# One encoder block on one core: u's low parts all by VectorE, tables loaded in pieces, v staged elsewhere, keys split 112 and 64

## What is computed

```python
hn = rms_norm(h, norm1_g[l])
q, k, v, u, g_na, g_ssm = jnp.split(hn @ w_in[l], IN_SPLITS, axis=-1)
y_na = neighbourhood_attention(q, k, v, na_rpb[l]).reshape(b, L, NA_WIDTH) @ w_proj_na[l]
y_ssm = s5_branch(u, ...) @ w_proj_ssm[l]
mixed = jax.nn.sigmoid(g_na) * y_na + jax.nn.sigmoid(g_ssm) * y_ssm
h = h + mixed @ w_out[l]
h = h + conv_gated_ffn(rms_norm(h, norm2_g[l]), w_up[l], conv_w[l], conv_b[l], w_down[l])
```

## Time and profile before

| | |
|---|---|
| median of 3 runs | 1456.84 us (1456.76 to 1457.27) |
| the profiled execution, its own time | 1456.88 us |
| its span, first to last instruction | 1455.0 us |
| busy: PE, DVE, ACT, POOL | 1432.3, 600.5, 663.3, 1014.2 us |
| mean granted TensorE clock | 0.997 |
| DMA | 271.48 MB, mean 187 GB/s |

### The profile page before, as it was taken

One profiled execution on the slowest core, in us unless ns is written; L12 is line 12 of the kernel. 1 busy time (PEld: TensorE's weight loads), 2 busy tenths in 40 slices (PEclk: granted clock), 3 DMA queues, 4 the chain that ended last, 5 costly groups with the idle time before them and its releaser, 6 DMA issues.

```text
span 1455.0 us, 30257 instructions
## 1 busy us (share of the span) xinstructions
PE 1432.3 (98%) x11735; PEld 1364.6 (94%) x11735; DVE 600.5 (41%) x1127; ACT 663.3 (46%) x897; POOL 1014.2 (70%) x475
## 2 busy tenths in 40 slices
PE   9899999999999999999999999999999999999997
PEld 9899999998998999999999999999999998888886
DVE  7858888887564265433322222222222221003002
ACT  6346444432454554454544444444444443334333
POOL 5000058840877788898888888888888887888885
PEclk9999999999999999999999999999999999999999
DMA  8896466656656455765565555655656555555553
GB/s 279 251 205 200 137 173 204 186 156 170 201 171 187 146 175 186 236 201 179 183 186 178 186 182 180 186 181 180 187 178 182 187 181 197 187 188 183 192 187 130
DMA packets 238304, 271.48 MB, mean 187 GB/s; under 512 B 21904, under 2 KB 224016, under 8 KB 237456
## 3 DMA queue, kind: packets, MB, share of 16 engines
q1 hardware_dynamic: 227968, 257.09, 57.9%
q10 hardware_dynamic: 10256, 13.26, 2.8%
HBM read 262.06 MB, written 8.26 MB: 186 GB/s over the span
## 4 chain that ended last, share of the span: by engine, by line
PE 80%; DVE 10%; DVEq 3%; issue 3%; DMA 2%; ACT 1%; POOL 1%; SPq 0%; ACTq 0%; POOLq 0%
PE ps L1470 20%; PE ps L1472 19%; PE ps L1471 19%; PE ps L1789 6%; PE ps L1791 6%; PE ps L1790 6%; DVE ps L1003 3%; DVE scan_states L1183 3%; DMA w_raw<-in_w_in 2%; DVEq L1182 2%; DVE w_lo L509 1%; POOL w_lo L509 1%; PE ps L1570 1%; PE ps L1627 1%; DVEq L1251 0%
## 5 line engine op out<-in xcount | busy, mean ns | idle before, releaser
L509 POOL TENSOR_TENSOR w_lo<-w_raw,w_hi 128x1024 fp32r<-128x1024 f32 x409 | 984.3, 2414 | 375.8 <-ACT w_hi L505 375.7
L505 ACT ACTIVATE w_hi<-w_raw 128x1024 fp32r<-128x1024 f32 x464 | 490.0, 1060 | 663.7 <-PE ps L1472 465.3
L1470 PE MATMUL ps<-act_hi,w_hi 128*128 128x258 f32 (+2 forms) x2432 | 695.4, 286 | 6.3 <-DVE w_lo L509 5.2
L1472 PE MATMUL ps<-act_hi,w_lo 128*128 128x258 f32 (+2 forms) x2432 | 690.5, 284 | 0.0
L1471 PE MATMUL ps<-act_lo,w_hi 128*128 128x258 f32 (+2 forms) x2432 | 689.4, 283 | 0.0
L1470 PEld LDWEIGHTS ps<-act_hi,w_hi 128*128 128x128 f32 x2432 | 461.2, 190 | 13.2 <-issue 8.5
L1471 PEld LDWEIGHTS ps<-act_lo,w_hi 128*128 128x128 f32 x2432 | 461.7, 190 | 0.1
L1472 PEld LDWEIGHTS ps<-act_hi,w_lo 128*128 128x128 f32 x2432 | 460.2, 189 | 0.0
L1789 PE MATMUL ps<-w_hi,hidden_hi 128*128 128x512 f32 x352 | 139.4, 396 | 0.0
L1791 PE MATMUL ps<-w_lo,hidden_hi 128*128 128x512 f32 x352 | 139.2, 396 | 0.0
L1790 PE MATMUL ps<-w_hi,hidden_lo 128*128 128x512 f32 x352 | 139.2, 395 | 0.0
(11 more groups left out here) (234 smaller groups left out, 1486.5 us busy)
## 6 DMA issues: line engine op xcount, KB each, us to landing
w_raw<-in_w_up SPq DMA_DIRECT2D x176, 512.0 KB, 3.5
w_raw<-in_w_in SPq DMA_DIRECT2D x128, 512.0 KB, 4.1
w_raw<-in_w_down SPq DMA_DIRECT2D x88, 512.0 KB, 3.7
w_raw<-in_w_out SPq DMA_DIRECT2D x32, 512.0 KB, 3.4
w_raw<-in_w_proj_na SPq DMA_DIRECT2D x16, 512.0 KB, 3.4
w_raw<-in_w_proj_ssm SPq DMA_DIRECT2D x16, 512.0 KB, 3.5
w_raw<-in_w_glu SPq DMA_DIRECT2D x8, 512.0 KB, 3.5
xT<-in_tokens ACTq DMA_DIRECT2D x1, 2176.0 KB, 9.1
```

The lines of the kernel that those rows point to most:

```text
L505: act.activation(slot(whi, k), slot(raw, k), ACT.Copy).then_inc(s_hi, 1)
L509: pool.tensor_tensor(slot(wlo, k), slot(raw, k), slot(whi, k).bitcast(F), ALU.subtract).then_inc(s_lo, 1)
L1470: mm(o, slot(whi, k)[:, cols], xh[:, kt, lo:lo + n], start=kt == 0, stop=False)
L1472: ins = mm(o, slot(wlo, k)[:, cols], xh[:, kt, lo:lo + n], start=False, stop=kt == units * UKT - 1)
```

## The change

It does these things:

- DVE makes the low parts of units 8 to 11 too, between its adds of squares; POOL no longer makes any before unit 51.
- The four parts of squares are added whole, tile by tile, with TENSOR_TENSOR (three adds of 128 x 1088, one of 544, one of 272) in place of four reductions and three adds. PE's `scale_sum` stands behind unit 8, `scale_transposes` behind unit 12 (before: 9 and 13).
- DVE's order over units 12 to 24 is another: low parts lie one to five places further ahead among the parameter steps, and `u_block(3)` comes earlier.
- Tables: b goes in four pieces of 512 KB after units 12, 13, 14 and 15, c in four pieces after units 40 to 43, before which SP waits for v's stores; `g_make(0)` waits for c.
- v's stage lies where `c_swapped` will be, so `s_copy(0)` waits for no store.
- Attention: keys are taken as 112 and 64. `probs_t` makes four transposes of 112 keys and two joint ones, each of the last 64 keys of one window and the first 64 of the other. `values` takes both windows' 112 keys first, then both windows' 64 keys, the two windows in different halves of the partitions. `att_load` has six DMAs. The multiply of `gate_na` goes from in front of the copies to behind `att_scores`.

The diff, cut to its core:

```diff
@@ memory, loads @@
-        vst = (at("v_stage_a", 29696, [P, 4, CB]), at("v_stage_b", 25600, [P, 4, CB]))
+        vst = (at("v_stage_a", 69120, [P, 4, CB]), at("v_stage_b", 73216, [P, 4, CB]))
-            eng.dma_start(va[:, j, :, :],
-                          v_d[:, 0:P, b * P:(b + 1) * P].rearrange("h p c -> p h c")).then_inc(s_qkv[j], 16)
-            eng.dma_start(vb[0:NB, j, :, :],
-                          v_d[:, P:WK, b * P:(b + 1) * P].rearrange("h p c -> p h c")).then_inc(s_qkv[j], 16)
+            for t in range(2):
+                eng.dma_start(va[0:KA, j, t, :], v_d[t, KEYS_A[t], b * P:(b + 1) * P]).then_inc(s_qkv[j], 16)
+                eng.dma_start(vb[KB * t:KB * (t + 1), j, :], v_d[t, KEYS_B[t], b * P:(b + 1) * P]).then_inc(s_qkv[j], 16)
@@ SP @@
-            load_in(U_U, 3 * HALF, 1, range(4, 6))
-            sp.wait_ge(s_nl, KT + SEED)
-            sp.wait_ge(s_xsq, 4)
-            table_load(R1, R2, b_rows)
-            load_in(U_U, 3 * HALF, 1, range(6, 8))
-            table_load(C1, C2, c_rows)
+            for k in range(8):
+                load_in(U_U, 3 * HALF, 1, (k,))
+                if k == 4:
+                    sp.wait_ge(s_nl, KT + SEED)
+                    sp.wait_ge(s_xsq, 4)
+                if k >= 4:
+                    table_load(0, k - 4)
...
-            for i in range(ITERS_IN):
-                load_in(U_K, HALF, i)
+            for u in range(16):
+                load_in(U_K, HALF, u // 8, (u % 8,))
+                if u == 8:
+                    for n in range(2):
+                        sp.wait_ge(s_vst[n], 16 * 4)
+                if 8 <= u < 12:
+                    table_load(1, u - 8)
@@ ACT @@
-            for q in range(4):
+            x_square(0)
+            x_square(1)
+            for q in range(2, 4):
+                hi_unit(act, U_U, 6 + q)
                 x_square(q)
-                hi_unit(act, U_U, 8 + q)
+            for k in range(10, 12):
+                hi_unit(act, U_U, k)
...
+            norm_root(0, L)
             hi_unit(act, U_U, 12)
-            norm_root(0, L)
@@ DVE @@
-            for q in range(4):
+            total = xsq[1]
+            for q in range(1, 4):
                 dve.wait_ge(s_xsq, q + 1)
-                dve.reduce_sum(sq[:, min(q, 1), :], xsq[q % 2][:, :, :].rearrange("p k t -> p t k"), AX.X)
+                dve.tensor_tensor(total[:, :, :], total[:, :, :], xsq[0][:, :, :], ALU.add).then_inc(s_xss, 1)
                 dve.drain()
-                if q:
-                    dve.tensor_tensor(sq[:, 0, :], sq[:, 0, :], sq[:, 1, :], ALU.add).then_inc(s_xss, 1)
-                    dve.drain()
-                else:
-                    dve.nop().then_inc(s_xss, 1)
+                if q < 3:
+                    lo(7 + q)
+            dve.tensor_tensor(sq[:, :, :], total[:, 0:2, :], total[:, 2:4, :], ALU.add)
+            dve.drain()
+            dve.tensor_tensor(sq[:, 0, :], sq[:, 0, :], sq[:, 1, :], ALU.add).then_inc(s_xss, 1)
+            lo(10)
+            lo(11)
...
                 if t == 0:
                     dve.wait_ge(s_vtp, 4 + SEED)
-                    for n in range(2):
-                        dve.wait_ge(s_vst[n], 16 * 4)
...
-                dve.tensor_copy(PA[:, :], ps[:, 4, :])
-                dve.tensor_copy(PB2[0:NB, :], ps[0:NB, 5, :]).then_inc(s_ptsb, 1)
+                dve.tensor_copy(PA[0:KA, :], ps[0:KA, 4, :])
+                dve.tensor_copy(PB2[:, :], ps[:, 5, 0:2 * P]).then_inc(s_ptsb, 1)
...
+                if b >= G_ATT - G_SCAN:
+                    n = b - (G_ATT - G_SCAN)
+                    dve.tensor_tensor(gate_na[:, 2 * n:2 * n + 2, :], gate_na[:, 2 * n:2 * n + 2, :],
+                                      rstd[:, LIVE:L].unsqueeze(1).to_broadcast([P, 2, NL]), ALU.mult).then_inc(s_gsc, 1)
                 att_norm(b)
@@ PE @@
-            product(U_U, 8, 4, hnh, hnl, 0, L, (4, 5), between=scale_sum)
+            product(U_U, 8, 4, hnh, hnl, 0, L, (4, 5), between=scale_sum, between_unit=0)
...
                 for ht in range(4):
-                    nc.tensor.transpose(ps[:, 4, P * ht:P * (ht + 1)], S[:, ht, 0:P], ident[:, :])
-                    ins = nc.tensor.transpose(ps[0:NB, 5, P * ht:P * (ht + 1)], S[:, ht, P:WK], ident[:, :])
+                    nc.tensor.transpose(ps[0:KA, 4, P * ht:P * (ht + 1)], S[:, ht, KEYS_A[ht % 2]], ident[:, :])
+                joint = S[:, :, :].rearrange("p h w -> p (h w)")
+                for hh in range(2):
+                    first = 2 * WK * hh + KA
+                    ins = nc.tensor.transpose(ps[:, 5, P * hh:P * (hh + 1)], joint[:, first:first + P], ident[:, :])
...
-                for t in range(2):
-                    for part in range(2):
+                for part in range(2):
+                    for t in range(2):
+                        other = slice(KB * t, KB * (t + 1))
                         for hh in range(2):
...
                             if part == 0:
-                                mm(o, va[:, j, t, hs], PA[:, col], start=True, stop=False, skip_group_check=True)
+                                mm(o, va[0:KA, j, t, hs], PA[0:KA, col], start=True, stop=False, skip_group_check=True)
                             else:
-                                ins = mm(o, vb[0:NB, j, t, hs], PB2[0:NB, col], start=False, stop=True,
+                                ins = mm(o, vb[other, j, hs], PB2[other, P * hh:P * (hh + 1)], start=False, stop=True,
```

More of the change, by code:

```diff
@@ L60 @@
 NB = WK - P
+KB = P // 2
+KA = WK - KB
+KEYS_A = (slice(0, KA), slice(KB, WK))
+KEYS_B = (slice(KA, WK), slice(0, KB))
 TWO_PI_HI = 6.28125
@@ L215, in encoder_block @@
         s_par = sem("params_loaded")
-        s_tab = sem("state_tables_loaded")
+        s_tab = [sem(f"state_tables_loaded_{n}") for n in "bc"]
         s_fg = sem("final_gain_loaded")
@@ L554, in _ @@
                     pool.drain()
-            pool.wait_ge(s_lo, 2 * DEPTH)
-            for k in range(2 * DEPTH, 3 * DEPTH):
-                lo_unit(pool, 0, k)
             pool.wait_ge(s_lo, U_Q + DEPTH - 1)
@@ L1023, in _ @@
             norm(0, L)
+            lo(12)
             u_block(0)
@@ L1091, in _ @@
             q_im = gq[:, 0, 1, :].unsqueeze(1).to_broadcast(three)
-            cmul((gq[:, 1:CHUNK, 0, :], gq[:, 1:CHUNK, 1, :]), (pw[:, 1:CHUNK, 0, :], pw[:, 1:CHUNK, 1, :]), (q_re, q_im),
-                 [prm[:, n:n + 3, :] for n in (0, 3, 6, 9)])
-            lo(20)
+            w_re, w_im = pw[:, 1:CHUNK, 0, :], pw[:, 1:CHUNK, 1, :]
+            parts = [prm[:, n:n + 3, :] for n in (0, 3, 6, 9)]
+            mul(parts[0], w_re, q_re)
+            mul(parts[1], w_im, q_im)
+            lo(22)
+            mul(parts[2], w_re, q_im)
+            mul(parts[3], w_im, q_re)
+            dve.drain()
+            dve.tensor_tensor(gq[:, 1:CHUNK, 0, :], parts[0], parts[1], ALU.subtract)
+            dve.tensor_tensor(gq[:, 1:CHUNK, 1, :], parts[2], parts[3], ALU.add)
+            dve.drain()
             for d in range(DIRS):
-                dq = slice(d * GROUPS, (d + 1) * GROUPS)
+                lo(23 + d)
+                dq = slice(GROUPS * d, GROUPS * (d + 1))
                 kin = pw[:, 1:CHUNK + 1, :, dq] if d else pw[:, CHUNK:0:-1, :, dq]
@@ L1136, in g_make @@
                 dve.drain()
-            for n in range(22, 32):
+            for n in range(25, 32):
                 lo(n)
-            dve.wait_ge(s_tab, 96)
+            dve.wait_ge(s_tab[0], 96)
             w_make(0)
@@ L1474, in half_unit, with product @@
                     ins.then_inc(s_used, 1)
-            def product(base_u, k0, units, xh, xl, lo, n, banks, split_before=None, split=s_nl, between=None):
+            def product(base_u, k0, units, xh, xl, lo, n, banks, split_before=None, split=s_nl, between=None, between_unit=1):
                 for q in range(units):
@@ L1482, in product @@
                         half_unit(base_u, k0 + q, q, units, m, xh, xl, lo, n, banks[m])
-                    if between and q == 1:
+                    if between and q == between_unit:
                         between()
```

51 lines of the change are left out of this document (25 added, 26 removed).

## The result

The changed kernel takes **1440.47 us** (median of 4 runs, 1440.03 to 1440.78), against 1457.05 (1456.76 to 1462.49) of the kernel before beside it: ratio 0.9877, 95% interval 0.9854 to 0.9900. The profiled run took 1440.03 us, with a span of 1437.9 (before: 1455.0), so 17.1 us have gone from the span.

The account below looks back on a forecast made before the run. PE, busy for 98% of the span, was taken to bound the kernel. Gains of 9.0 + 2.2 + 1.7 + 3.9 = 16.8 us off 1456.9 gave 1440.1 us, range 1438.0 to 1448.0.

Parts of the forecast that it names:

- The start stretch: PE up to unit 24: 5.6 us of waits, 1.6 for seven stops and 1.7 of low clock go, sum 9.0.
- The low clock: Shortly after PE's wait before unit 16, clock 0.50 for 3.4 us; with no stop before it, 1.7 us go.
- Attention, waits: Attention blocks: the gate_na multiply moved behind the scores ends three waits of PE, 2.2 us (1.7 to 2.6).
- Transposes: Attention: two fewer transposes of 0.105 us each in eight blocks, 1.7 us.
- values: Attention: the new grouping takes 0.98 us per block for 1.47, 3.9 us in eight blocks (at most 4.5).
- v's stage: Where s_copy(0) waited for v's stores PE has no wait of its own: nothing won, cost 0.
- The scan: DVE's 67 steps begin with PE's last chunk product and keep their distance: 0.
- (a): The start keeps part of its waits, shrunk to half: gain 8 to 12 us in all, 1445 to 1449; chance 0.13.
- (b): Attention: the moved gate_na multiply delays probabilities, PE waits 1 to 1.5 us in six blocks: 1448; chance 0.06.
- (c): Attention: the packing doesn't pay, values as before: 1444.0; chance 0.08 beyond the main case.
- (d): Slower: DVE falls behind, PE stops at every unit from 12 to 24; 1460 if unit 21's low part comes at 93; chance 0.02.
- (e): Start: the clock's low stretch merely moves, another transfer takes table c's place in the queue: 1454 to 1457; chance 0.03.

Follow-up runs that it names:

- experiment 3: Kernel before plus squares added whole, low parts of units 8 to 11 on DVE, sum behind unit 8, table c whole behind unit 40: 1451.06 us.
- experiment 4: Changed kernel with DVE's old order of low parts and parameter steps over units 12 to 24: 1441.07 us.
- experiment 5: Changed kernel with table c's four pieces back in front of unit 16 and v's stage in its old place: 1444.81 us.
- experiment 1: Kernel before with table c alone moved, loaded whole behind unit 40's load: 1452.18 us.
- experiment 10: Changed kernel with the old keys of 128 and 48 and values window by window: 1445.95 us.
- experiment 9: Changed kernel with the old keys of 128 and 48, values still both windows' first parts, then their second parts: 1443.04 us.
- experiment 6: Changed kernel with v's stage alone back in its old place, with the waits for its stores: 1440.08 us.
- experiment 8: Changed kernel with values taken window by window again, keys still 112 and 64: 1448.52 us.
- experiment 11: Changed kernel with the four copies into the eye table made behind unit 24's low part instead of behind the scan: 1438.83 us.

## Why the prediction was right, point by point

*The start stretch,* 9.0 predicted, 8.9 measured from unit 8 to unit 24. Its steps: adds of 1.28 to 1.29 us (taken 1.3); the product with the ones at 35.35 (35.8); `u_block(1)` done at 42.83 (43.6) and unit 12 at 44.88 (45.5), of which 0.46 is the start-up; low parts 16 to 21 done at 51.7, 55.6, 60.1, 62.8, 65.6 and 68.7 (52.4, 56.0, 60.6, 63.0, 66.0, 69.1); the least margin 3.5 us, at unit 18 (3.6); unit 24 at 82.6 (83). Unit 16's load was issued at 40.14 (40.8) and landed at 49.03, well within the 12.88 us that I allowed. The terms come out too: the seven stops of the kernel before make 5.7 us of waits and 1.6 of lost overlap, and the 1.6 that are left of 8.9 are the low clock (1.7).

*Which part of the change earned it* was not worked out in the prediction. The traces divide the stretch from unit 8 to unit 24, which lasts 59.2 us before and 50.3 after. The early sum and the late table c make it 52.9 (experiment 3: 6.3 saved), the tables in pieces 51.0 (experiment 4: 1.9 more), and the new order of DVE's list 50.3 (0.8 more). Table b in pieces, which had no price of its own in the prediction, is thus worth more than the order written by hand. For that 1.9 I take it that table c, late in both, and v's stage do nothing between units 8 and 24; no kernel with table b whole and the rest changed was run.

*The low clock.* I counted 1.7 us for it "with no stop before it". The stretch is gone from the changed kernel's trace. But experiment 5 keeps its clock at 1.0 through a stop of 3.25 us, and experiment 1 has no low stretch while it keeps five shorter stops. The term came out; the reason, that the stop brings the fall, does not hold each time, and what decides it is open. In that the term was lucky.

*Attention, waits,* 2.2 predicted. In the trace of the kernel before, blocks in which PE is not held last 14.96 us, and the four in which it waits for the scores last 15.17, 15.42, 15.72 and 15.71: 2.2 us more in all. Put back into the changed kernel the multiply costs 3.6, since the blocks are shorter there. The two don't contradict each other: taken away from the kernel before it is worth 2.2 by these rows, added to the changed one 3.6.

*Transposes,* 1.7, and *values,* 3.9: together 5.6, experiment 10 gives 5.5. By the rows, eight transposes take 0.96 us and six 0.75, and the values 1.47 and 0.97. The groups' starts are 0.58 and 0.38 apart (0.61 and 0.37). The guess that side-by-side passes on quarters need a step of 0.12 and a change of shape 0.25 also gives 2 x (0.36 + 0.25) = 1.22 for experiment 9, where 1.17 was measured. The Trainium skill, page "TensorEngine Tiling (Array Packing)", section "Key Properties", says that changing the tiling mode drains TensorE while changing the tile alone does not. The groups agree: the same number of passes takes 1.47 us with four changes and 1.17 with two.

*v's stage,* 0: experiment 6 shows it. *The scan,* 0: it lasts 115.5 and 115.4 us in the two traces.

*The rivals.* (a) The start keeps waits: none kept. (b) The multiply collides: I had priced it as always waiting for POOL, 2.4 us. It takes 0.68 to 0.70 us in four of its six blocks, 1.92 and 1.87 in the other two, and the scaling behind it 0.97 in block 5, with nothing waiting; the kernel with it in front is slower in every run. But the collision that I feared for the scaling is real, in experiment 8. (c) The packing does not pay: it does. (d) and (e) have nothing for them.

*The range:* its three bounds add up to 1.4 us, which gives 1438.7 on the low side and not 1438.5; the range is the same.

*The sum:* 16.8 predicted; 16.6 between the medians. That it is so near is partly luck. The medians of the kernel before in the experiments would make it 17.1 to 17.5. Between the two profiled runs it is 16.85, but 0.46 of that is the start-up, which the change does not touch.

## What to carry to other kernels

Before a stage where one engine is never to stop, look at the DMA queue in order: 2 MB of tables in front of one weight load cost 3.7 us here, nearly as much as the five other late low parts with their stops (4.3), and the cure was to load them later and in pieces. Moving an instruction of an engine that is busy half the time pays when it stands in front of what the busy engine waits for, and the gain grows as the busy engine gets faster. When a wait is gone, look at the ones that are left: moving four small copies and two gate blocks brought 5.1 us, as much as a third of the whole change, a part of it by pauses in the scan that went unasked. And a gain of one part alone is not its share: the early sum and the late table c both got rid of the same low clock.

## What the runs showed of the hardware that I had not expected

*A DVE instruction can lose to POOL several times in a row.* In the changed kernel each of the first two scalings of block 1 lasts as long as one low part of POOL (2.56 and 2.45 us beside 2.4) and then gets in. In experiment 8 one waited 11.5 us, through two low parts, four bias rows and two more low parts, until POOL had a gap of 0.19 us. The Trainium skill, page "SBUF — State Buffer", section "Summary: rules for kernel authors", says that when VectorE runs in a mode of two ports, or reads two SBUF tensors while the GpSimd instruction reads SBUF, the second of the two to issue fully blocks until the first has finished. In which mode the scaling ran no row shows. The first case agrees with that rule; the second goes on past the end of the first instruction, and there the measurement decides: such a meeting can cost more than one instruction of POOL, here all of them up to its next gap. Why DVE got in between two low parts in the first case and not in the second is open.

*The same instructions can run with or without pauses.* The steps of the scan take 115.4 us in the changed kernel with its four pauses, 114.8 in experiment 6 where these are shorter, and 114.1 in experiment 11 where there are none. A change in front of a long serial stretch can so gain or lose a microsecond that no account of its own work contains.
